# A two-layer streaming encoder on one core: inputs, input projection, queries and keys in one block written out by hand, and another order inside the delta stage

## The chip, the cores and the metric

The kernel runs on one core of one Trainium2 chip. The metric is the time of one execution on the device in microseconds (us), the median of the runs shown. The profile is one further execution of the same program. TensorE (PE) does the matrix products, ScalarE (ACT), VectorE (DVE) and GpSimd (POOL) the elementwise work, and SyncE (SP) issues the DMAs.

## What is computed

One inference step of a two-layer encoder for 1024 prompt tokens and 64 sample tokens that share the weights. Cut to what matters here:

```python
# layer 0, mixer
h = x @ w_in                                   # x (tokens, 1024), w_in (1024, 2208)
c_q, c_kv, k_r, gate_b, gate_c, sh = split(h)  # 384, 256, 32, 512, 512, 512
q   = rms_norm(c_q, g_q) @ w_uq                # 8 heads of 64 + 32; rope on the 32
lat = rms_norm(c_kv, g_kv)                     # output p_latent / s_latent
kr  = rope(k_r)                                # output p_krope / s_krope
kv  = concat(past_lat, lat) @ w_ukv            # keys and values of 8 heads
o_att = chunk_attention(q, k, v)
o_sc  = gate_b * causal_dwconv(gate_c * sh)    # 3 taps
x = layer_norm(ALPHA * x + concat(o_att, o_sc) @ w_o);  x = layer_norm(ALPHA * x + conv_ffn(x))
# layer 1, mixer: gated delta rule in chunks of 64 tokens, 8 heads of 128
#   per chunk: m = tril(k b k^T * decay), solve (I + m) sol = rhs, then
#   v_new = w - k_cd S;  o = q_dec S + attn v_new;  S = S g + k_tail^T v_new
```

All is float32. A product of float32 rank is made of three products of rounded parts: high by high, low by high, high by low.

## The kernel before

**Layout.** Features lie on the 128 partitions and tokens along the free dimension: 1092 columns (1024, a gap of 4, 64), in three thirds of 364 (`SPLIT`), each third one PSUM bank. `TILES` are nine tiles of 128 tokens (the last of 64). Every operand exists as a rounded part `hi` and a rest `lo`. `mm3` (lines 142 to 151) issues the three matmuls of one product. A *unit* of weights is 1024 x 128 numbers: SP loads it into `wraw` (three slots), POOL makes `whi` (L134) and `wlo` (L138) of it, and PE multiplies it with all tokens in 3 x 8 x 3 = 72 matmuls. The 18 units of the input projection are kv0, kv1, kr, q0, q1, q2 (the `head`) and four times gc, sh, gb.

**Blocks.** The program is a row of blocks; no engine goes into the next one before all have ended the present one. Semaphores of a block are cleared by POOL (L97) as the next one closes.

- `inputs_block`: SP issues 16 small loads of parameters, then nine tiles of x; PE waits for the small loads (`rows_in`), transposes them (L240), then transposes x, eight 128 x 128 pieces a tile (L253); ACT rounds the tile to `xhi` (L265), DVE subtracts to `xlo` (L273) and scales to `z` (L275). At the end all of `z` goes to the tensor `residual` in one DMA.
- `even_in_block`: the 18 units; ACT and DVE evacuate `ps`; DVE does the short convolution of each gc, sh, gb group (L539 to L563).
- `queries_block`: squares on ACT, sums over partitions with a matrix of ones on PE (L639), Sqrt on ACT (L617), reciprocal on DVE (L661), scaling (L664), `qhi` and `qlo`, 216 matmuls with `w_uq`, evacuated to `qT` (L628), and the rotation (rope) of `krf` and of each head on DVE: shuffle, two products, one sum (L684 to L690).
- `keys_block`: the cached latents are loaded and transposed (L754), the new ones are transposed back to rows and stored (L762, L835), then the keys (ACT to `kT` L814 and `kpast` L816) and the values (DVE to `V`, L839). POOL copies the rotated `krf` to the eight heads of `kT` (L743).
- `attention_block`, then `out_ffn_block` and a layer norm, then layer 1: `odd_in_block`, `gates_block`, `delta_block`, `out_ffn_block`, layer norm. The final layer norm writes the outputs.

**The delta stage.** `delta_block` walks over pairs of chunks. In one `run(A, B, C)` on each engine, pair A is prepared, pair B (the one before) is put through the state S, and the gates of C are made ready. The engines' programs are written out in a fixed order. For A: `kn` scales the keys (L2461), `gram_k` on PE fills bank 6, from which DVE makes `T` (L2468), `TT` (L2470), `MT` (L2471), and adds the identity to `TT` (L2476) and `T` (L2477); `AT` comes from bank 7 (L2480); `kturned` (L2222) transposes the keys into banks 6 and 7, from which DVE makes `ktl` (L2487) and ACT `kbg` (L2377). Then five levels: `X = T^T ML` (PE L2274, banks 4 and 5, copied by ACT L2388), then two products into banks 6 and 7 (L2287, L2290), which DVE subtracts from `T` and `TT` (L2504, L2505). For B: `vn` (L2442), a step of the state (PE L2185, DVE L2448), twice, and the squares of the output (ACT L2382). Before the first level PE waits for the second `S` (`pe.wait_ge(s("S"), B.th(3, 2))`).

## Time and profile before

| what | us |
|---|---|
| median of 3 runs (lowest, highest) | 3386.13 (3385.78, 3389.47) |
| the profiled execution's own time | 3385.98 |
| its span, first to last instruction | 3384.2 |
| PE busy | 3093.8 |
| POOL busy | 1053.3 |
| DVE busy | 1582.2 |
| ACT busy | 718.0 |

The span is the time between the first and the last instruction in the trace; 1.8 us lie around it. Busy times are sums of instructions and overlap between engines. The granted clock is the share of TensorE's full speed that it was allowed; half is 1.2 GHz, full is 2.4 GHz.

### The profile page before, as it was taken

The page shows a single profiled execution, that of the slowest core. Times are in us where ns is not written, and L with a number is a line of the kernel's source. Part 1 is how long each engine was busy: PE and PEld are TensorE (multiplying, and loading weights), DVE is VectorE, ACT ScalarE, POOL GpSimd, SP SyncE. Part 2 cuts the span into 40 slices and gives each one's busy share as a digit, 9 for nine tenths or more (in the row PEclk, how much of TensorE's full clock was granted, in tenths as well). Part 3 has the DMA queues.
Part 4 walks back from the last instruction along what each step waited for, and adds up shares of the span by engine and source line. Part 5 has one row for each costly group of instructions (what it writes and reads, how often), then busy time and mean ns, then how long its engine had stood idle before and what let it go on. Part 6 is the DMA issues. An engine that isn't in the chain of part 4 may idle for free. (4 is left out here: it accounts for less than half of the span.)

```text
span 3384.2 us, 54266 instructions
## 1 busy us (share of the span) xinstructions
PE 3093.8 (91%) x22776; PEld 2932.2 (87%) x22776; DVE 1582.2 (47%) x2716; ACT 718.0 (21%) x1349; POOL 1053.3 (31%) x708
## 2 busy tenths in 40 slices
PE   5997799999999999995999948988799999999996
PEld 4996666999999999983999947777689999999995
DVE  2127376463434434443666645555164444434444
ACT  1002267130010100103112224444031110100102
POOL 1220110343222233203232236666425233222220
PEclk8998899999999999997999979999799999999998
DMA  4100110211111111102233223331401111111101
GB/s 148 44 24 18 31 44 2 85 38 48 40 44 44 38 44 57 38 1 91 78 96 96 77 72 82 85 77 37 144 13 54 40 44 57 38 44 44 38 26 54
DMA packets 251736, 184.15 MB, mean 54 GB/s; under 512 B 47695, under 2 KB 236477, under 8 KB 251269
## 3 DMA queue, kind: packets, MB, share of 16 engines
q1 hardware_dynamic: 251525, 181.09, 17.9%
q8 instruction: 162, 2.65, 0.3%
q14 instruction: 49, 0.40, 0.0%
HBM read 147.19 MB, written 33.84 MB: 53 GB/s over the span
## 5 line engine op out<-in xcount | busy, mean ns | idle before, releaser
L145 PE MATMUL ps<-xhi,whi 128*128 128x364 f32 (+1 forms) x3528 | 1165.7, 330 | 88.0 <-POOL wlo L138 68.4
L146 PE MATMUL ps<-xlo,whi 128*128 128x364 f32 (+1 forms) x3528 | 1163.6, 330 | 0.0
L151 PE MATMUL ps<-xhi,wlo 128*128 128x364 f32 (+1 forms) x3528 | 1162.7, 330 | 0.0
L145 PEld LDWEIGHTS ps<-xhi,whi 128*128 128x128 f32 (+1 forms) x3528 | 662.0, 188 | 94.8 <-POOL wlo L138 69.1
L146 PEld LDWEIGHTS ps<-xlo,whi 128*128 128x128 f32 (+1 forms) x3528 | 662.2, 188 | 4.3 <-issue 0.8
L151 PEld LDWEIGHTS ps<-xhi,wlo 128*128 128x128 f32 (+1 forms) x3528 | 661.8, 188 | 3.4 <-issue 0.6
L1540 DVE TENSOR_TENSOR z<-ps,z 128x364 f32<-128x364 f32 x528 | 283.3, 537 | 640.3 <-PE ps L151 640.3
L1310 POOL TENSOR_SCALAR whi<-wraw 128x1024 fp32r<-128x1024 f32 x136 | 149.1, 1096 | 1036.2 <-PE ps L151 1034.6
L1313 POOL TENSOR_TENSOR wlo<-wraw,whi 128x1024 fp32r<-128x1024 f32 x136 | 349.0, 2566 | 11.3
L134 POOL TENSOR_SCALAR whi<-wraw 128x1024 fp32r<-128x1024 f32 (+3 forms) x56 | 57.0, 1019 | 497.2 <-PE ps L145 229.3
L145 PE MATMUL ps<-oo_hhi,whi 128*128 128x364 f32 x528 | 173.8, 329 | 0.3 <-DVE z L1540 0.3
L145 PE MATMUL ps<-eo_hhi,whi 128*128 128x364 f32 x528 | 173.8, 329 | 0.3 <-DVE z L1540 0.3
L151 PE MATMUL ps<-eo_hhi,wlo 128*128 128x364 f32 x528 | 173.6, 329 | 0.0
L151 PE MATMUL ps<-oo_hhi,wlo 128*128 128x364 f32 x528 | 173.6, 329 | 0.0
L146 PE MATMUL ps<-eo_hlo,whi 128*128 128x364 f32 x528 | 173.2, 328 | 0.0
L146 PE MATMUL ps<-oo_hlo,whi 128*128 128x364 f32 x528 | 173.2, 328 | 0.0
L138 POOL TENSOR_TENSOR wlo<-wraw,whi 128x1024 fp32r<-128x1024 f32 (+3 forms) x56 | 133.7, 2388 | 4.7
L1756 DVE SCALAR_TENSOR_TENSOR oin_conv<-oin_raw,par,oin_conv 128x1092 f32<-128x1092 f32 x72 | 109.0, 1514 | 10.5 <-DVE oin_conv L1752 0.2
L145 PEld LDWEIGHTS ps<-eo_hhi,whi 128*128 128x128 f32 x528 | 99.3, 188 | 0.6 <-DVE z L1540 0.6
L145 PEld LDWEIGHTS ps<-oo_hhi,whi 128*128 128x128 f32 x528 | 99.3, 188 | 0.6 <-DVE z L1540 0.6
L146 PEld LDWEIGHTS ps<-oo_hlo,whi 128*128 128x128 f32 x528 | 99.2, 188 | 0.0
L146 PEld LDWEIGHTS ps<-eo_hlo,whi 128*128 128x128 f32 x528 | 99.2, 188 | 0.0
(376 smaller groups left out, 4294.4 us busy)
## 6 DMA issues: line engine op xcount, KB each, us to landing
wraw<-in_w_ff_in SPq DMA_DIRECT2D x88, 512.0 KB, 3.8
wraw<-in_w_ff_out SPq DMA_DIRECT2D x44, 512.0 KB, 3.5
qkvz<-oin_out SPq DMA_DIRECT2D x32, 546.0 KB, 2.8
wraw<-in_w_in_o SPq DMA_DIRECT2D x32, 512.0 KB, 4.3
residual<-z SPq DMA_DIRECT2D x2, 4368.0 KB, 11.8
z<-residual SPq DMA_DIRECT2D x6, 1456.0 KB, 9.8
wraw<-in_w_in_e SPq DMA_DIRECT2D x17, 512.0 KB, 3.8
dn_gb<-gates SPq DMA_DIRECT2D x34, 128.0 KB, 3.4
```

The lines of the kernel that those rows point to most:

```text
L134: pool.tensor_scalar(m.whi[:, k, 0:cols], m.wraw[:, r, 0:cols], 1.0, 1.0, ALU.mult, ALU.mult)\
L138: pool.tensor_tensor(m.wlo[:, k, 0:cols], m.wraw[:, r, 0:cols], m.whi[:, k, 0:cols].bitcast(F32), ALU.subtract).then_inc(s("w_lo"), 1)
L145: one = pe.matmul(out, whi, xhi, start=start, stop=False)
L146: two = pe.matmul(out, whi, xlo, start=False, stop=False)
L151: return pe.matmul(out, wlo, xhi, start=False, stop=stop)
L1310: pool.tensor_scalar(hi, m.wraw[:, n % RAW, :], 1.0, 1.0, ALU.mult, ALU.mult).then_inc(s("w_hi"), 1)
L1313: pool.tensor_tensor(lo, m.wraw[:, n % RAW, :], hi.bitcast(F32), ALU.subtract).then_inc(s("w_lo"), 1)
L1540: dve.tensor_tensor(m.z[:, o, SPLIT[q]], m.ps[:, 6 + seq % 2, 0:NS], m.z[:, o, SPLIT[q]], ALU.add)\
L1756: dve.scalar_tensor_tensor(cv[:, :], x[:, 1 + t:1 + t + TW], one("dconv", t), cv[:, :], ALU.mult, ALU.add).then_inc(s("taps"), 1)
```

## The change

The blocks for inputs, input projection, queries and keys become one, `front_block`, with no loop in it. In it x is loaded first; after every three tiles of x one third of the unit kv0 is multiplied; the parameters come behind the first two units; `ALPHA * x` goes tile by tile through the buffer `zt` to `residual`. The latents' sums of squares are made by one matmul with ones each, after DVE has added the squares, and stand between the units, as do the transposes of the latents; the root is Exp(-0.5 Ln), with no reciprocal. The queries follow the last unit, the keys the queries (both now in two sets of banks), and the values the keys (four banks). Buffers share their places, so that some loads wait (the tables `cos` and `sin` for the short convolution's end). The rows of `kr` are turned and stored at once (`krows`).

In `delta_block` the first level's X goes to banks 0 and 1, ACT makes `vb` before `eg` and the squares of the output after the first X, DVE multiplies bank 6 in place and makes `T` from it in one sum out of PSUM, adds the identity to `TT` later, and PE starts `kcd` half by half.

```diff
--- before.py
+++ after.py
-def inputs_block(nc, ctx, m, d):
-def even_in_block(nc, ctx, m, d):
-def queries_block(nc, ctx, m, d):
-def keys_block(nc, ctx, m, d):
+def front_block(nc, outer, m, d):
...
+        PAIR = [4, 6, 2, 4, 6, 2, 4, 6, 4]
...
+            x_tile(0)
+            x_tile(1)
+            x_tile(2)
+            weight(0)
+            x_tile(3)
+            weight(1)
+            x_tile(4)
+            x_tile(5)
+            z_tile(0)
+            z_tile(1)
+            x_tile(6)
+            weight(2)
+            for t in (7, 8):
+                z_tile(t - 5)
+                x_tile(t)
...
+            sp.wait_ge(s("osc"), NT)
+            sp.wait_ge(s("st_done"), NT)
+            sp.dma_start(cos[rr, :], d["rope_cos"]).then_inc(s("tables"), 16)
+            sp.dma_start(sin[rr, :], d["rope_sin"]).then_inc(s("tables"), 16)
...
+            def turn_x(t):
+                n = TILES[t][1]
+                pe.wait_ge(s(f"x_in{t}"), 16)
+                if t >= 3:
+                    last = t - 3 if t < 8 else 6
+
+                    pe.wait_ge(s(f"zt{last % 2}"), last // 2 + 1)
+                for k in range(KD):
+                    ins = pe.transpose(tile_psum(t)[:, k, :], xin[0:n, t % 4, k * P:(k + 1) * P], m.ident[0:n, 0:n])
...
+            for t in (0, 1, 2):
+                turn_x(t)
+            pe.wait_ge(s("lo_x"), 3)
+            gemm(0, 0)
+            for t in (3, 4, 5):
+                turn_x(t)
+            pe.wait_ge(s("lo_x"), 6)
+            gemm(0, 1)
+            for t in (6, 7, 8):
+                turn_x(t)
+            pe.wait_ge(s("lo_x"), 9)
...
+            for n in range(2, NU):
+                for q in range(SPL):
+                    gemm(n, q)
+                if 3 <= n < 6:
+                    sum_of_squares(n - 3)
+                if 7 <= n < 10:
+                    sum_of_squares(n - 4)
+                if 8 <= n < 17:
+                    turn_latent(n - 8)
...
+                    elif h == 1:
+                        pe.wait_ge(s("q_free"), SPL * HEADS)
+                        if q == 2:
+
+                            pe.wait_ge(s("krows"), 1)
...
+            act.preload_act_table_set(LN_EXP)
+            for step in ("h0", "h1", "h2", "z0", "h3", "h4", "z2", "h5", "h6", "z4", "h7", "z6", "h8", "z8"):
+                (high if step[0] == "h" else scaled)(int(step[1]))
...
+            for t in range(9):
+                low(t)
+                if t % 2:
+                    scaled(t)
...
+            dve.wait_ge(s("tables"), 32)
+            for h in range(HEADS):
+                rope(h)
+            dve.wait_ge(s("kr_turned"), 1)
+            dve.tensor_copy(krows[:, 0:NTOK, :], m.ps[:, 6, 0:NTOK * ROPE].rearrange("p (t r) -> p t r", r=ROPE))
+            dve.tensor_copy(krows[0:DEC, NTOK, :], m.ps[0:DEC, 6, NTOK * ROPE:9 * ROPE]).then_inc(s("krows"), 1)
+            rope(HEADS)
...
+    X_BANK = [None, 0] + [4] * (LEVELS - 2)
...
                     if B:
-                        pe.wait_ge(s("S"), B.th(3, 2))
-                    else:
-                        pe.wait_ge(s("vb"), A.th(1, 1))
-
+                        pe.wait_ge(s("vn"), B.th(B.nb, 2))
                     for l in range(1, LEVELS):
                         pe.wait_ge(s("ML"), A.th(l, LEVELS - 1))
+                        if l == 2:
+
+                            if B:
+                                pe.wait_ge(s("S"), B.th(3, 2))
...
-                    pe.wait_ge(s("TT"), A.th(A.group(LEVELS - 1, A.nb - 1), 2 * LEVELS))
                     pe.wait_ge(s("vb"), A.th(1, 1))
...
                     for b in range(A.nb):
+                        pe.wait_ge(s("TT"), A.th(A.group(LEVELS - 1, b), 2 * LEVELS))
+                        settle(pe, s("settled_pe"))
...
-                if B:
-                    act.wait_ge(s("o"), B.th(len(B.blocks()), 2))
-                    act.activation(sq[:, :, 0:B.n], bank2(2, B.n), ACT.Square).then_inc(s("osq"), 1)
+                if B and not A:
+                    squares_o(B)
...
-                            act.copy(X[:, hs, :], bank1(4 + b)[:, hs, :]).then_inc(s("Xs"), 1)
+                            act.copy(X[:, hs, :], bank1(X_BANK[l] + b)[:, hs, :]).then_inc(s("Xs"), 1)
+                        if B and l == 1:
+                            squares_o(B)
```

On TensorE, at the start of the program, the order before is the following (`ptmp` holds the parameters' rows, `xin` the tiles of x; in brackets the semaphores waited for).

```order
L240 MATMUL ps<-ident,ptmp 128x114 [waits in_rows_in,in_consts]
L240 MATMUL ps<-ident,ptmp 128x66 x2
L240 MATMUL ps<-ident,ptmp 128x72
L240 MATMUL ps<-ident,ptmp 128x96
L240 MATMUL ps<-ident,ptmp 128x64
L253 MATMUL ps<-ident,xin 128x128 [waits in_x_in0]
```

At the same place now, with the first product right behind three tiles:

```order
L444 MATMUL ps<-ident,fr_xin 128x128 [waits fr_x_in0,fr_ident]
L444 MATMUL ps<-ident,fr_xin 128x128 x7
L444 MATMUL ps<-ident,fr_xin 128x128 [waits fr_x_in1]
L444 MATMUL ps<-ident,fr_xin 128x128 x7
L444 MATMUL ps<-ident,fr_xin 128x128 [waits fr_x_in2]
L444 MATMUL ps<-ident,fr_xin 128x128 x7
L145 MATMUL ps<-xhi,whi 128x364 [waits fr_w_lo,fr_lo_x]
```

The parameters no longer stand ahead of x, and the first matmul of kv0 waits for three tiles and its weights instead of nine tiles, the residual's store and a block's end.

On VectorE, in the part behind the last unit of the projection, the order now is this (`fr_osc` is the short convolution's result, `fr_llo` the latents' rest, `fr_turned` the rotation's buffer, `fr_tables` the semaphore of the loads of cos and sin).

```order
L787 TENSOR_TENSOR fr_osc<-fr_gc,fr_gb 128x1092 [waits fr_free0,fr_conv]
L846 TENSOR_TENSOR fr_plo<-ps,fr_phi 128x2x128 [waits fr_osc,fr_st_done,fr_past_hi]
L846 TENSOR_TENSOR fr_plo<-ps,fr_phi 128x2x128 [waits fr_past_hi]
L849 COPY strow<-ps 16x128 [waits fr_z_gap_out]
L853 TENSOR_TENSOR fr_llo<-fr_ckv,fr_lhi 128x1092 [waits fr_lat_turned,fr_lhi] x2
L799 STREAM_SHUFFLE fr_turned<-fr_krf 32x1092 [waits fr_tables]
L800 TENSOR_TENSOR fr_turned<-fr_krf,fr_cos 32x1092
L802 TENSOR_TENSOR fr_turned<-fr_turned,fr_sin 32x1092 [waits fr_swapped]
L805 TENSOR_TENSOR fr_krf<-fr_turned 32x1092 [waits fr_sind,fr_cosd]
```

Norms, reciprocals and `qlo` no longer stand between the last unit and the rotations, but the tables' loads and the latents' rest do.

On VectorE in a full `run` of the delta stage the order before is:

```order
L2468 TENSOR_TENSOR dn_T<-ps,dn_low 128x512
L2470 TENSOR_TENSOR dn_TT<-ps,dn_upl 128x512
L2471 TENSOR_TENSOR dn_MT<-ps,dn_ups 128x512
L2448 TENSOR_TENSOR dn_S<-ps,dn_Sg 128x1024
L2476 TENSOR_TENSOR dn_TT<-dn_TT,masks 128x512
L2477 TENSOR_TENSOR dn_T<-dn_T,masks 128x512
L2480 TENSOR_TENSOR dn_AT<-ps,dn_upi 128x512
```

The same place now:

```order
L2666 TENSOR_TENSOR dn_TT<-ps,dn_upl 128x512
L2667 TENSOR_TENSOR dn_MT<-ps,dn_ups 128x512
L2670 TENSOR_TENSOR ps<-ps,dn_low 128x512
L2645 TENSOR_TENSOR dn_S<-ps,dn_Sg 128x1024
L2675 TENSOR_TENSOR dn_T<-ps,masks 128x512
L2678 TENSOR_TENSOR dn_AT<-ps,dn_upi 128x512
L2639 TENSOR_TENSOR dn_vn<-dn_kbg,ps 128x512
L2682 TENSOR_TENSOR dn_TT<-dn_TT,masks 128x512
```

The sum that ends in `T` now reads PSUM, and the one that ends in `TT` has moved behind `AT` and the second `vn`.

## Rows read from the trace of the kernel before

**Rows 1.** The page: TensorE's busy tenths and granted clock in 40 slices

```profile
PE   5997799999999999995999948988799999999996
PEclk8998899999999999997999979999799999999998
```

**Rows 2.** Timeline, 0 to 60 us: start, duration, engine, what, [idle before <-releaser]

```profile
6.97 3.79 SPq L213 DMA_DIRECT2D xin<-in_x_prompt  x8
8.02 1.22 PE L240 MATMUL ps<-ident,ptmp 114*128 114x114 f32 x6 [8.02 <-DMA dtb<-in_dt_bias]
...
12.23 1.01 ACT L265 CAST xhi<-ps 128x1024 fp32r<-128x1024 f32 x1 [2.08 <-PE ps L253]
13.35 1.23 DVE L273 TENSOR_TENSOR xlo<-ps,xhi 128x1024 fp32r<-128x1024 f32 x1 [13.35 <-ACT xhi L265]
...
44.95 12.68 SPq L120 DMA_DIRECT2D wraw<-in_w_in_e  x6
...
49.13 1.04 POOL L134 TENSOR_SCALAR whi<-wraw 128x1024 fp32r<-128x1024 f32 x1 [2.80 <-DMA wraw<-in_w_in_e]
50.26 2.34 POOL L138 TENSOR_TENSOR wlo<-wraw,whi 128x1024 fp32r<-128x1024 f32 x1
...
52.65 0.67 PE L145 MATMUL ps<-xhi,whi 128*128 128x364 f32 x1 [27.06 <-POOL wlo L138]
```

**Rows 3.** One line each, evacuations of the units: min/median/max ns, first and last start

```profile
L506 ACT COPY ckv<-ps x3: 462/462/463, 59.1 to 67.1; 128x364 f32<-128x364 f32 x3
L517 ACT COPY ein_gb<-ps x12: 462/463/464, 154.9 to 270.7; 128x364 f32<-128x364 f32 x12
```

**Rows 4.** One line each, between the last unit and attention

```profile
L639 PE MATMUL ps<-q_sq,ones x30: 469/814/976, 276.8 to 300.4; 128*128 128x364 f32 x30
L628 ACT COPY qT<-ps x24: 457/459/462, 313.2 to 347.8; 96x364 f32<-96x364 f32 x24
L690 DVE TENSOR_TENSOR qT<-q_turned x8: 1286/1287/1289, 320.8 to 357.8; 32x1092 f32<-32x1092 f32 x8
L814 ACT COPY kT<-ps x24: 455/456/457, 379.7 to 408.5; 64x364 f32<-64x364 f32 x24
L839 DVE COPY V<-ps x11: 683/692/693, 410.6 to 424.5; 128x512 f32<-128x512 f32 x10, 64x512 f32<-64x512 f32 x1
L1023 ACT ACT_TABLE_LOAD  x1: 1283/1283/1283, 427.9 to 427.9; - x1
```

**Rows 5.** Timeline, 424 to 432 us: TensorE's first work in the attention block

```profile
425.54 0.62 PE L935 MATMUL ps<-kpast,qT 96*64 96x256 f32 x2 [1.05 <-PEq L702]
```

**Rows 6.** One line each: VectorE on two-input or SBUF work, beside GpSimd and alone

```profile
L563 DVE TENSOR_TENSOR osc<-ein_gc,ein_gb x4: 1297/1913/1915, 163.5 to 271.3; 128x1092 f32 x4
L743 POOL COPY kT<-krf x8: 1086/1090/1094, 373.6 to 380.9; 32x1092 f32<-32x1092 f32 x8
```

**Rows 7.** Timeline of the delta stage, 2140 to 2186 us, VectorE

```profile
2147.60 2.38 DVE L2477 TENSOR_TENSOR dn_T<-dn_T,masks 128x512 f32<-128x512 f32 x1
...
2153.15 1.22 DVE L2448 TENSOR_TENSOR dn_S<-ps,dn_Sg 128x1024 f32<-128x1024 f32 x1
```

**Rows 8.** The same stretch, TensorE, ScalarE and GpSimd

```profile
2150.84 1.06 PE L2222 MATMUL ps<-ident,dn_k 128*128 128x128 f32 x8 [0.46 <-DVE dn_AT L2480]
...
2154.51 1.15 PE L2274 MATMUL ps<-dn_T,dn_ML 64*64 64x64 f32 x32 [0.67 <-DVE dn_S L2448]
2156.43 0.95 PE L2287 MATMUL ps<-dn_X,dn_TT 64*64 64x64 f32 x16 [0.78 <-ACT dn_X L2388]
...
2174.48 2.00 PE L2305 MATMUL ps<-dn_TT,dn_kbg 64*128 64x64 f32 x32 [0.61 <-DVE dn_TT L2505]
...
2152.83 2.17 ACT L2377 ACTIVATE dn_kbg<-ps,bcol 128x128 f32<-128x128 f32 x8 [8.39 <-DVE dn_ktl L2487]
...
2147.08 2.35 POOL L2113 TENSOR_TENSOR dn_Sg<-dn_S,dn_egl 128x1024 f32<-128x1024 f32 x1
```

**Rows 9.** Windows: length, busy (x instructions) PE, PEld, DVE, ACT, POOL, clock, DMA, GB/s

```profile
2061.12:2101.22 40.10, 36.28 (x730) 31.83 (x730) 23.03 (x35) 20.39 (x42) 28.22 (x18) 1.00 0.31 81
```

More of the change, by code:

```diff
@@ new lines, in gemm @@
+            def gemm(n, q):
+                kind, t = UNITS[n]
+                g, i = group(UNITS[n])
+                cols = wide(kind)
+                hi, lo = halves_of(n)
+                pe.wait_ge(s("w_lo"), n + 1)
+                if i >= 1:
+                    pe.wait_ge(s(f"free{g}"), SPL * (i - 1) + q + 1)
+                for k in range(KD):
+                    w = slice(k * cols, (k + 1) * cols)
+                    ins = mm3(pe, m.ps[0:cols, 3 * g + q, 0:NS], hi[:, w], lo[:, w], m.xhi[:, k, SPLIT[q]],
+                              m.xlo[:, k, SPLIT[q]], k == 0, k == KD - 1)
+                ins.then_inc(s(f"full{g}"), 1)
@@ L262, in _ @@
             ins.then_inc(s("params_done"), 1)
[L263 to L265 removed]
+            evacuate(("kr", 0), krf[rr, :])
+            squares(0)
+            root(0)
+            squares(1)
+            evacuate(("q", 1), cq[:, 1, :])
+            root(1)
+            squares(2)
+            root(2)
+            squares(3)
+            gate(0)
+            root(3)
@@ new lines, in _ @@
+            squares(4)
+            evacuate(("gb", 0), gb)
+            root(4)
+            squares(5)
+            latent_row(0)
+            gate(1)
+            root(5)
+            for k in range(KKV):
+                act.wait_ge(s("normed"), normed_count(SPL))
+                act.copy(lhi[:, k, :], ckv[:, k, :]).then_inc(s("lhi"), 1)
+            latent_row(1)
+            for k in range(KQ):
+                act.wait_ge(s("normed"), normed_count(2 * SPL))
+                act.copy(qhi[:, k, :], cq[:, k, :]).then_inc(s("qhi"), 1)
```

904 lines of the change are left out of this document (486 added, 418 removed).

## The prediction

> **What bounds the kernel now.** I read the page first. TensorE's row of tenths shows a 5 in the first slice of 84.6 us and two 7s in the fourth and fifth, then 9 nearly throughout up to the last third; it is the engine that the rest waits for [rows 1]. So I looked for its holes and for what ends them.
>
> The timeline of the first 60 us gives the first hole. The small loads stand ahead of x in SP's queue: x is issued at 6.97, TensorE starts at 8.02 behind the last small load, ACT rounds the first tile at 12.23. The first product starts at 52.65, after 27 us of idleness that the weights' `wlo` ends; the weights were issued only at 44.95, once the residual had been stored and the block had ended [rows 2]. From there to the last unit TensorE has no hole: the evacuations of a unit's thirds come 4.0 us apart (59.1 to 67.1 is two steps), so a unit costs 12.0; the first third costs more, since 52.65 to 67.1 is 14.45 for what takes 12.0 later (clock at half: 2.4 us) [rows 2, 3].
>
> The second hole lies between 270.7 (last evacuation of the last unit) and 425.5 (first work of attention): 154.8 us [rows 3, 5]. The lines in it show what it holds: sums of squares to 300.4, the first query evacuated at 313.2, the last at 347.8, rotations to 357.8 and 1.3 more, the first key evacuated at 379.7, the last at 408.5, values to 425.2 [rows 4]. The products alone are 36 + 30 + 16 us; some 70 us are waits in a row.
>
> The third is the delta stage. One full pair takes 40.1 us with TensorE busy for 36.3 [rows 9]. Its own waits in a pair are short: 0.46, 0.67, 0.78 and 0.61 us [rows 8], but what it does in between is stretched by an order in which VectorE's chain comes first.
>
> **The change, part by part.**
>
> *Head.* x is issued first, at about 0.8. From issue to rounding it takes 12.23 - 6.97 = 5.3, so the first rounding is at 6.1; the last of three tiles needs 1.0 on ACT and four steps of VectorE (three `xlo`, one scaled tile) of 1.2 [rows 2]: 12.0. The weights are fourth in the queue: 4.2 from issue to GpSimd's start before (44.95 to 49.13), some 8.3 now, and 1.04 + 2.34 for the split gives 11.7 [rows 2]. First third 12.0 to 16.0. The next three tiles are turned only then: 1.1 for eight transposes (1.06 for eight of this size in [rows 8]), 1.0, and four steps of 1.2: product at 22.9 to 26.9. The last three tiles are in series with the scaling that frees their banks and with the store that frees `zt` (an ACT step, a transposition, an ACT step, and about 3 us for a store): 9.8, product at 36.7. Two thirds of a unit (8.0) being done, it is as if the projection had begun at 28.7, against 52.65: **24.0 us** gained. The half-speed start of 2.4 is paid in both.
>
> *Between the units* TensorE gets six sums at 0.47 (the shortest of L639) [rows 4], 2.8, six parameter transposes (0.8) and 18 latent transposes (0.13 each by [rows 8] and a start for each of nine pairs, estimated at 3.2): 6.8 us added. Their partners on ACT and VectorE have a whole unit of 12 us each; the longest queue ahead of one (convolution, product, norm, sum after gb0) is some 9 us by durations like those in [rows 6], so I cost their waits at nothing; without that cover each would cost its excess over 12.
>
> *Behind the last unit*, at U: five transposes, 1. Queries: 34.6 us for 23 steps [rows 4], 1.5 each, 24 of them, 36.1: U+37.1. Small transposes: U+38.7. A head of keys takes 3.7 (28.8 us for nearly eight, less the slow start) [rows 4]; head 0 and two thirds of head 1 end at U+44.4, and there TensorE waits for `krows`, which stands behind eight rotations on VectorE. Those: the convolution's last product beside GpSimd 1.9 [rows 6], from U+0.7, so U+2.6 (the tables, issued then, land by about U+5.5); the past's rests and the copy 1.2; the latents' two rests 1.3 each and 0.6 each lost beside GpSimd's split, U+7.6. A rotation comes every 5.28 us (37.0 / 7 in L690) [rows 4], eight are 42.3. GpSimd makes its eight copies of 1.09 into `kT` meanwhile [rows 6]; about five two-input steps fall into that time and lose 0.6 each (1.91 against 1.30) [rows 6]: 3. With two copies 0.5: U+53.4. So TensorE stands for 9.0 us, and what was late next is the keys: 24.1 left, 2.0 for a clock at half after the pause, U+79.5; values 15.9 as before, 0.3 to attention: U+95.7. With the 6.8 that is 102.5 against 154.8: **52.3** gained. What is gone here are norms, reciprocals, Sqrt, two block ends, two loads and a row-by-row store.
>
> The first exponential of attention no longer waits for its table, 1.28 [rows 4]: **1.3**.
>
> *Weighing a rule.* The sum into `T` takes 2.38 us for 512 columns, where `S` out of PSUM takes 1.22 for 1024; it starts while GpSimd's `Sg` runs from 2147.08 to 2149.43 and ends 0.55 after it [rows 7, 8]. The Trainium skill, SBUF — State Buffer, section "Who interferes with whom", says that a VectorE instruction with two SBUF inputs is fully blocked by a GpSimd instruction that reads SBUF, and that one with a single SBUF input is not. By this rule the new sum out of PSUM is free of it, and the trace agrees with the 2.38. It speaks against the front, though: five rotation steps would each lose a copy's 1.09, not 0.6, and `krows` come 2.5 later; the total would be 3289 instead of 3286.
>
> *Delta.* Relative to `kn` at 2141.20. VectorE: `TT`, `MT`, the in-place product and `T` out of PSUM at 0.7 each (an estimate from 1.22 for `S`, twice as wide), the last in place of 2.38 [rows 7], `AT`, `vn`: the second `vn` comes about 1.8 earlier. But TensorE's own queue was done only 0.46 before `kturned` at 2150.84 [rows 8]; the earlier `vb` moves that queue by some 0.4 more, so only 0.8 of the 1.8 arrives there, at 2150.0. `kbg` then starts at 2152.0 instead of 2152.83. Level one no longer waits for the second `S` (end of 2153.15 + 1.22): it starts near 2153.0, not 2154.51, and ACT copies X before it squares B's output, which takes about 1 us out of the 1.4 between `kbg`'s end (2155.0) and the next product. `kbg` ends at 2154.1, X is copied by 2154.5, the next product starts there instead of at 2156.43: **1.9**. `kcd` waits for the first half of `TT` alone: the wait of 0.61 goes [rows 8]. 2.5 per pair; eight full stages 20, the first stage (no B) about 2: **22**. `TT`'s identity sum, two SBUF inputs, now stands beside GpSimd; it may lose up to 1.3, and the 1.0 between it and `kturned` hides most of that. GpSimd is busy 28 of 40 us [rows 9]; everything it does starts as much earlier.
>
> Sum: 24.0 + 52.3 + 1.3 + 22 = 99.6. From the profiled execution's 3385.98: **3286**; that execution lies 0.15 under the median of the runs, so the figure stands for it too.
>
> **Rivals.**
> - *Better tail and steadier clock* (0.22): the pause at `krows` is as short as the rotations alone make it (4.8 off), no half clock behind it (2.0), and the added transposes are paid by half (3); delta gains 3 per pair. Another 13: 3273. For it: the stretches with a full clock in [rows 1]. Against: TensorE's pauses of this size were followed by half speed at 52.65 [rows 2, 3].
> - *Delta gives little* (0.15): the pair is held by TensorE's own 36.3 of 40.1 [rows 9]; if only the waits shown go (0.61 + 0.67), 8 x 1.3 = 10. 12 less: 3298.
> - *A slower head* (0.10): x, nine stores of 512-byte pieces and weights share SP's queue, and TensorE works in bursts there, so half speed is paid for two thirds more (2 x 4) and a store or load comes 4 late: 3298.
> - *Slower than before* (0.02): the small steps between the units drop the clock to 1.2 GHz for the projection. A unit then costs 24 instead of 12 (the half-speed start shows matmuls taking twice as long). From 8.3 of the 18 units on, the whole gain is gone; with all of them the time is 3502. Against it: the projection runs at full clock through [rows 1]'s third slice, and the added steps are 0.5 us.
> - *It does not do what it says* (0.01): the steps between the units are held by ACT's and VectorE's queues, 15 of them at 6.6 us each, about the 100 that the rest gives: 3386. For it: ACT and VectorE each serve all of them in one order. Against: a unit's 12.
> - My forecast as worked out, 3278 to 3294: 0.50.
>
> **How the numbers follow.** The likeliest case gives 3286. The range reaches over the better tail and over the two weaker cases: 3267 to 3304; outside I leave 2 in 10. 0.2% is 6.8 us, about what a measurement of this kernel tells from none; all cases but two are far beyond it on the fast side: faster 0.97, same 0.01, slower 0.02.
>
> **What would show it.** In the changed profile: first L145 near 12 us, with holes behind each third until about 37; no hole longer than 1 us from there to the last unit near 253; a wait for `krows` of 5 to 11 us about 44 us behind it; attention's first matmul near 349; `dn_T` out of PSUM at 0.7 us and a pair every 37.5 us. I am wrong if TensorE waits at the sums between the units, if half clock shows inside the projection, or if the pair stays at 40.

## The result and the profile after

The changed kernel takes 3305.93 us (median of 4 runs, 3305.22 to 3307.16) against 3387.8 for the kernel before (4 runs beside them, 3385.78 to 3389.59): ratio 0.9753, 95% interval 0.974 to 0.9767. It is 82 us faster, where I had forecast 100: the time lies 20 us above the 3286 and just above my range. The profiled execution's span fell from 3384.2 to 3304.5, by 79.7; the accounts below are made with spans.

The page's two rows for TensorE look like those of [rows 1]; only the start is better filled.

```profile
PE   7998999999999999985999949998899999999996
PEclk8999999999999999997999979998899999999998
```

The timeline of the first 50 us shows what took the place of the hole of [rows 2]: three bursts of products, each behind a pause.

```profile
4.91 4.68 PE L444 MATMUL ps<-ident,fr_xin 128*128 128x128 f32 x24 [4.91 <-DMA fr_xin<-in_x_prompt]
...
13.18 0.67 PE L145 MATMUL ps<-xhi,whi 128*128 128x364 f32 x1 [3.60 <-DVE xlo L724]
...
19.89 1.91 PE L444 MATMUL ps<-ident,fr_xin 128*128 128x128 f32 x16
...
27.39 0.67 PE L145 MATMUL ps<-xhi,whi 128*128 128x364 f32 x1 [2.36 <-DVE xlo L724]
...
33.86 1.03 PE L444 MATMUL ps<-ident,fr_xin 128*128 128x128 f32 x8
...
42.49 1.02 ACT L604 ACTIVATE fr_zt<-ps 128x1024 f32<-128x1024 f32 x1 [3.37 <-DMA residual<-fr_zt]
43.66 1.09 PE L444 MATMUL ps<-ident,fr_xin 64*128 64x64 f32 x8 [5.58 <-ACT fr_zt L604]
...
46.15 0.67 PE L145 MATMUL ps<-xhi,whi 128*128 128x364 f32 x1 [1.40 <-DVE xlo L724]
```

The thirds of the first unit begin at 13.18, 27.39 and 46.15 (forecast 12.0, 22.9, 36.7). The first two last 6.7 and 6.5 us, not 4.0. The windows over the same stretch (busy time of PE, PEld, DVE, ACT, POOL, then PEclk, DMA share, GB/s) say why: the clock is near its half level, 1.2 GHz, in both.

```profile
13.00:20.00 7.00, 6.82 (x25) 6.80 (x26) 0.13 (x1) 0.00 (x0) 3.16 (x2) 0.57 1.14 284
20.00:27.00 7.00, 2.87 (x25) 2.42 (x23) 4.38 (x4) 3.87 (x4) 1.14 (x2) 0.91 0.31 77
27.00:34.00 7.00, 6.61 (x26) 6.58 (x27) 1.56 (x2) 0.00 (x0) 0.00 (x0) 0.60 0.87 228
```

The waits of TensorE between the last unit (its last product ends at about 261.9) and the start of attention:

```profile
PE ps L145 <- DVE fr_krows L860: 13.0, 1, 13.0
PE ps L1139 <- ACT att_p L1213: 3.3, 1, 3.3
PE ps L1125 <- PEq L256: 1.1, 1, 1.1
```

I had 9.0 for the first and nothing for the second. Added up by stretches of the two spans (forecast, measured):

| stretch | forecast | measured | missed |
|---|---|---|---|
| start to the last unit's end | ends at 253.5 | 261.9 | 8.4 |
| last unit to attention's first product | 95.7 | 98.5 | 2.8 |
| attention to its last result | 1.3 gained | 171.8 against 168.6, 3.2 lost | 4.5 |
| attention's last result to the first `kn` | nothing | 1431.6 against 1428.5 | 3.1 |
| first to last `kn` (delta) | 22 gained | 302.1 against 322.0, 19.9 gained | 2.1 |
| last `kn` to the end | nothing | 1038.6 against 1039.6 | -1.0 |

The misses add up to 19.9, and 99.6 - 19.9 is the 79.7.

### The profile page after: what moved, and what is told of

Read it like the earlier page. It is cut to its first block and busy times, and to the rows that moved or that the text cites. A ratio compares the mean times of both kernels' runs of the same rounds, so it can differ in the third digit from the quotient of the medians.

```text
span 3304.5 us, 54021 instructions
## 1 busy us (share of the span) xinstructions
PE 3082.5 (93%) x22758; PEld 2930.9 (89%) x22758; DVE 1582.0 (48%) x2701; ACT 722.6 (22%) x1346; POOL 1062.7 (32%) x708
## 5 line engine op out<-in xcount | busy, mean ns | idle before, releaser
L1503 POOL TENSOR_TENSOR wlo<-wraw,whi 128x1024 fp32r<-128x1024 f32 x136 | 349.4, 2569 | 11.3
L134 POOL TENSOR_SCALAR whi<-wraw 128x1024 fp32r<-128x1024 f32 (+1 forms) x33 | 34.7, 1052 | 248.6 <-DMA wraw<-in_w_in_o 132.0
L151 PEld LDWEIGHTS ps<-oo_hhi,wlo 128*128 128x128 f32 x528 | 99.1, 188 | 0.0
```

Source lines behind the costliest of these rows:

```text
L134: pool.tensor_scalar(m.whi[:, k, 0:cols], m.wraw[:, r, 0:cols], 1.0, 1.0, ALU.mult, ALU.mult)\
L151: return pe.matmul(out, wlo, xhi, start=False, stop=stop)
L1503: pool.tensor_tensor(lo, m.wraw[:, n % RAW, :], hi.bitcast(F32), ALU.subtract).then_inc(s("w_lo"), 1)
```

## The experiments

Sixteen kernels. "Changed" is the kernel under study at 3305.93 us; medians are of 4 or 5 runs. Two things limit how finely they can be read: the same head code brings the last unit's end to anywhere from 258.6 to 261.9, and eleven kernels with the same new delta stage have stretches from first to last `kn` of 301.4 to 307.5 us (mean 304.3). Below 3 us I read nothing from one profile. The changed kernel's own profile is at the late end of that head, so comparisons of the head with it flatter what they test. And the kernel before, run again beside each group of experiments, had medians of 3389.55 to 3392.85 us where it had 3387.8 beside the changed kernel: a difference of two medians from different groups is uncertain by 2 to 5 us, and the ratios, each taken against the kernel before in its own group, are the better guide there.

| label | us | ratio to before (95%) | span |
|---|---|---|---|
| e_delta | 3367.92 | 0.9938 (0.9917 to 0.9959) | 3366.0 |
| e_front | 3327.89 | 0.9818 (0.98 to 0.9835) | 3322.5 |
| e_krows | 3290.01 | 0.9705 (0.9687 to 0.9724) | 3287.1 |
| e_gap | 3299.32 | 0.9735 (0.9717 to 0.9753) | 3294.4 |
| e_order | 3303.35 | 0.9742 (0.9729 to 0.9756) | 3301.6 |
| e_zbuf | 3302.04 | 0.9739 (0.9725 to 0.9752) | 3300.3 |
| e_warm | 3300.39 | 0.9731 (0.9718 to 0.9745) | 3300.2 |
| e_kg | 3283.32 | 0.9683 (0.967 to 0.9696) | 3279.8 |
| e_eo | 3301.74 | 0.9734 (0.9718 to 0.9751) | 3298.3 |
| e_best | 3271.42 | 0.9641 (0.9624 to 0.9657) | 3270.7 |
| e_noT | 3304.76 | 0.9744 (0.9727 to 0.976) | 3305.7 |
| e_noX | 3315.8 | 0.9774 (0.9755 to 0.9793) | 3313.9 |
| e_dve | 3312.12 | 0.9768 (0.9755 to 0.9782) | 3309.9 |
| e_noVB | 3309.02 | 0.9754 (0.974 to 0.9767) | 3307.6 |
| e_noKCD | 3309.36 | 0.9758 (0.9744 to 0.9771) | 3311.2 |
| e_pool | 3298.18 | 0.9724 (0.971 to 0.9737) | 3301.7 |

**The two halves: e_delta and e_front.** The edit is the function `delta_block` of one kernel in the other, nothing else.

> The kernel before with the delta stage of the changed one and nothing else. The stretch from the first kn to the last was 19.9 us shorter in the changed kernel's trace. If the delta orders are worth that by themselves, and the front only shifts them: 19 to 22 us under the kernel before, about 3367. Rival: part of the 19.9 came with the clock or with what the front leaves behind, then the two parts do not add up and this gives 12 or less.

> The changed kernel with the delta stage of before, so the new front alone. If the parts add up: 3306 + 20 = 3326, 61 us under the kernel before, where my prediction had 24.0 + 52.3 + 1.3 = 77.6. Rival: the front is worth its 77.6 and it is the two together that lose 16 us; then this gives about 3310.

By spans the delta stage alone gives 18.2 and the front alone 61.7: 79.9 together, against 79.7 for both at once. The ratios say the same (21 and 62 us of 3387.8). They add up, the rivals (12 us or less, and about 3310) are out, and the miss lies in the front: 61.7 where I had 77.6. That the sum agrees to 0.2 is chance: e_delta's head came 2.1 later than in the kernel before with the same instructions, and e_front's last unit ended 3.3 earlier than the changed kernel's.

**The stall at `krows`: e_krows.**

```diff
-            for h in range(HEADS):
+            for h in range(5):
                 rope(h)
             dve.wait_ge(s("kr_turned"), 1)
...
-            rope(HEADS)
+            for h in range(5, HEADS + 1):
+                rope(h)
```

> The changed kernel with the two copies of krows on VectorE put behind the fifth rotation instead of the ninth-but-one; the rotations themselves and everything else as they are. Theory: TensorE's 13.0 us of idleness behind the second head's keys is the queue ahead of these copies; the fifth rotation ends at 301.5, TensorE needs the bank at 304.7, so the 13.0 goes, and 1 to 2 us of half clock behind it: 13 to 15 us faster than the changed kernel, about 3292. Rival: what is late next (the last rotations, the copies of the keys on ACT, GpSimd's copies) takes most of it: 3299 or more.

The copies now run at 300.8, the wait for `fr_krows` is gone from the list of waits, and from the last unit to attention it takes 83.1 us instead of 98.5: 15.4 less: 13.0 of wait, and 2.4 for the clock, which was granted at 0.50 and 0.65 from 316 to 324 us behind the wait and is at 1.00 throughout now. The median is 16 lower. Nothing takes the stall's place.

**A part of why the stall was 13.0 and not 9.0: e_pool.**

```diff
-            pool.wait_ge(s("roped"), 1)
+            pool.wait_ge(s("roped"), HEADS)
             for h in range(HEADS):
                 pool.tensor_copy(m.kT[rr, h, :], krf[rr, :]).then_inc(s("kr"), 1)
```

> The changed kernel with GpSimd's eight copies of the turned key rows waiting for the eighth rotation, so that no rotation runs beside them. In the changed kernel the first two query rotations and part of the third take 2.0 to 2.2 us a step where the later ones take 1.28: seven steps lose 5.2 us together, where I had put 3. Theory: the krows copies come 5.2 us earlier and the pause of 13.0 us on TensorE shrinks to 7.8; the copies are done long before attention: 5 us faster, 3301. Rival: GpSimd is still splitting weights beside the rotations, or its copies now hold the V memset and with it the values: no gain.

The timeline of the changed kernel: one of GpSimd's copies beside VectorE's shuffle and three beside its next steps (each asked for by itself; the timeline of a longer stretch merges them), the rotation of VectorE beside them, and one later:

```profile
276.04 1.09 POOL L426 COPY kT<-fr_krf 32x1092 f32<-32x1092 f32 x1 [3.89 <-DVE fr_krf L805]
...
278.12 2.16 POOL L426 COPY kT<-fr_krf 32x1092 f32<-32x1092 f32 x1
280.23 2.15 POOL L426 COPY kT<-fr_krf 32x1092 f32<-32x1092 f32 x1
282.33 2.16 POOL L426 COPY kT<-fr_krf 32x1092 f32<-32x1092 f32 x1
...
277.34 1.98 DVE L800 TENSOR_TENSOR fr_turned<-qT,fr_cos 32x1092 f32<-32x1092 f32 x1
279.25 2.18 DVE L802 TENSOR_TENSOR fr_turned<-fr_turned,fr_sin 32x1092 f32<-32x1092 f32 x1
281.53 2.00 DVE L805 TENSOR_TENSOR qT<-fr_turned 32x1092 f32<-32x1092 f32 x1
...
292.32 1.27 DVE L800 TENSOR_TENSOR fr_turned<-qT,fr_cos 32x1092 f32<-32x1092 f32 x1
293.52 1.28 DVE L802 TENSOR_TENSOR fr_turned<-fr_turned,fr_sin 32x1092 f32<-32x1092 f32 x1
294.90 1.29 DVE L805 TENSOR_TENSOR qT<-fr_turned 32x1092 f32<-32x1092 f32 x1
...
317.32 0.43 DVE L859 COPY fr_krows<-ps 128x256 f32<-128x256 f32 x1
```

And of the kernel with the copies later, the first query rotation and the wait:

```profile
277.26 1.27 DVE L800 TENSOR_TENSOR fr_turned<-qT,fr_cos 32x1092 f32<-32x1092 f32 x1
278.46 1.28 DVE L802 TENSOR_TENSOR fr_turned<-fr_turned,fr_sin 32x1092 f32<-32x1092 f32 x1
```

```profile
PE ps L145 <- DVE fr_krows L860: 8.6, 1, 8.6
```

The stall shrank by 4.4 where I expected 5.2; the way from the last unit to attention by 3.8, the median by 7.8. The missing 0.8 is the seventh slow step, which I had put down to the copies: it is the rotation of `krf` at 271.21, beside GpSimd's last splitting of weights, and it takes 2.06 us in e_pool too. The third query rotation was not slowed in either. So the copies slow six steps and cost 4.4, where the prediction had put 3 for five; that part of `krows`' lateness is shown.

**Attention's start: e_gap.**

```diff
         def _(dve):
...
             masks, adds = [0], [0]
+            for hp in range(HP):
+                dve.memset(attended(hp)[:, SEQ:S0], 0.0).then_inc(s("gap"), 1)
...
         def _(pool):
-            for hp in range(HP):
-                pool.memset(attended(hp)[:, SEQ:S0], 0.0).then_inc(s("gap"), 1)
```

> The changed kernel with attention's four small memsets of the gap columns moved from GpSimd to the head of VectorE's program. Theory: ACT's first exponential at 366.13 waits for these memsets, and they stand on GpSimd behind some 70 clears of the front's semaphores (360.3 to 365.9); without it the exponential starts about 3.3 to 4.5 us earlier: 3301.5 to 3302.7. Rival: something else that GpSimd's or the block's end holds (scores, maximum) is due at the same time: no difference, 3306.

In the kernel before the first exponential starts 3.70 us behind TensorE's first product at 425.54, its table's 1.28 included:

```profile
429.24 0.52 ACT L1023 ACTIVATE att_p<-ps,att_ng 64x320 f32<-64x320 f32 x1
```

In the changed kernel's timeline it waits for a memset of four columns, which GpSimd reaches 5.5 us after TensorE has begun:

```profile
360.40 0.62 PE L1125 MATMUL ps<-fr_kpast,qT 96*64 96x256 f32 x2 [1.05 <-PEq L256]
...
365.99 0.11 POOL L1334 MEMSET att_o<- 128x4 f32 x1
366.13 0.52 ACT L1213 ACTIVATE att_p<-ps,att_ng 64x320 f32<-64x320 f32 x1 [21.72 <-POOL att_o L1334]
...
366.89 1.06 PE L1139 MATMUL ps<-ident,att_p 64*128 64x64 f32 x6 [3.29 <-ACT att_p L1213]
```

With the memsets on VectorE the exponential follows the maximum at once:

```profile
359.30 0.62 PE L1125 MATMUL ps<-fr_kpast,qT 96*64 96x256 f32 x2 [1.05 <-PEq L256]
...
361.72 0.52 ACT L1213 ACTIVATE att_p<-ps,att_ng 64x320 f32<-64x320 f32 x1 [18.42 <-DVE att_ng L1273]
...
364.83 1.06 POOL L1337 TENSOR_SCALAR whi<-wraw 128x1024 fp32r<-128x1024 f32 x1 [42.67 <-issue]
```

It starts 2.4 us behind TensorE's first product instead of 5.7; from that product to attention's last result it takes 166.4 instead of 171.8: 5.4, of which 3.3 is the wait and 2.1 the clock behind it (granted at 0.52 and 0.50 from 367 to 373 us, at 1.00 in e_gap). GpSimd still does nothing else for 5.5 us (359.3 to 364.8). What it does there is the clearing of the front's semaphores (`Sems.close`, L97). The clears of this place, in the changed kernel and then in the kernel before:

```profile
L97 POOLq EVENT_SEMAPHORE_RANGE_CLEAR  x78: 44/44/48, 360.3 to 365.8; - x78
```

```profile
L97 POOLq EVENT_SEMAPHORE_RANGE_CLEAR  x22: 44/44/44, 425.5 to 426.9; - x22
```

78 clears take 5.5 us and 22 took 1.4.

**Both: e_kg.** The two edits together.

> Both moves together on the changed kernel: the copies of krows behind the fifth rotation, and attention's gap memsets on VectorE. Alone they measured 16 to 17 us and 6 to 10 us (spans 3287.1 and 3294.4 against 3304.5), of which I take 15.4 and 5.4 as theirs, by the stretches that they touch, and the rest as chance of the head's clock. If they are independent: 21 us under the changed kernel, span about 3283.5. Rival: both live off the same pause of TensorE, and together they give no more than the first alone, 3290.

22.6 by median, 24.7 by span, where 21 was expected. The two stretches are as in the kernels with one edit each: 83.2 us from the last unit to attention (83.1 in e_krows), 166.3 through attention (166.4 in e_gap). They are independent; the rest of the 24.7 is spread of the head and of other stretches.

**The head: e_order, e_zbuf, e_warm.** The first moves one step of ACT, and on SP the small loads behind the residual's stores; the second gives each of the nine scaled tiles its own buffer (on ACT, VectorE and SP alike); the third puts 108 transposes of the identity into six holes of TensorE, 26, 12, 14, 12, 36 and 8 of them (the first place is shown).

```diff
-            for step in ("h0", "h1", "h2", "z0", "h3", "h4", "z2", "h5", "h6", "z4", "h7", "z6", "h8", "z8"):
+            for step in ("h0", "h1", "h2", "z0", "h3", "h4", "z2", "h5", "z4", "h6", "h7", "z6", "h8", "z8"):
```

```diff
-                if t >= 2:
-                    act.wait_ge(s("z_out0"), 16 * (t // 2))
-                act.activation(zt[:, 0, :, 0:n], tile_psum(t), ACT.Copy, scale=ALPHA).then_inc(s("zt0"), 1)
+                act.activation(z_buf(t), tile_psum(t), ACT.Copy, scale=ALPHA).then_inc(s("zt0"), 1)
```

```diff
+            def warm(bank, n):
+                for _ in range(n):
+                    pe.transpose(m.ps[:, bank, 0:P], m.ident[:, :], m.ident[:, :])
...
             for t in (0, 1, 2):
                 turn_x(t)
+            warm(0, 26)
             pe.wait_ge(s("lo_x"), 3)
             gemm(0, 0)
```

> The changed kernel with two moves in the head: ACT scales tile 4 ahead of rounding tile 6 (not behind it), and SP issues the sixteen small loads behind the residual's stores (not ahead of tile 4's). Theory: the third group of tiles is late because the scaled tiles queue up behind their stores, two buffers deep; tile 4's store then goes out some 6 us earlier, and the second unit third's product starts at 40 to 42 instead of 46.2: 4 to 6 us faster, 3300 to 3302. Rival: the stores are held by the 16 DMA engines, not by their place, and land no earlier: within 2 us of 3306.

> The changed kernel with a buffer of its own for each of the nine scaled tiles (in memory that the query latents take later), so that no scaling waits for a store; orders on all engines unchanged. Theory: with the two DMA waits of 3.37 and 3.70 on ACT and VectorE gone, x's last tile is turned at about 40.3 and the third product starts near 43 instead of 46.2: 3 to 4 us faster, about 3302.5. Rival: what is late there is the clock and the order, not the store: under 1.5 us.

> The changed kernel with 108 transposes of the identity by itself put into TensorE's six holes between 8 and 46 us (26, 12, 14, 12, 36 and 8 of them), into banks that the next product overwrites; nothing waits for them. Theory: the thirds of the first unit take 6.7 and 6.5 us instead of 4.0 because the clock is at half behind each hole; with TensorE busy in the holes they run at full clock and 5 to 7 us of the head go: about 3300. Rival: the clock falls whatever fills the holes, or the fillers themselves come in the way: 3306 or more.

The third product starts at 41.51, 41.38 and 41.55 instead of 46.15. But in the other kernels with the head unchanged it starts anywhere from 42.82 (e_front) to 45.99 (e_pool), so that only 1.3 us of the 4.6 is sure to come from the edit. The last unit ends at 258.0 and 257.0 for the first two, against 258.6 to 261.9; the medians fell by 2.6 and 3.9, less than the 4 to 6 that I gave the order. What is shown is the wait itself: in e_order ACT's scaling of tile 6 waits 0.80 us for a store, not 3.37 (1.7 to 3.1 in the other kernels); in e_zbuf not at all. With the holes filled the windows over the changed kernel's three stretches become:

```profile
13.00:20.00 7.00, 7.00 (x52) 6.98 (x52) 0.83 (x1) 1.88 (x3) 3.05 (x2) 1.00 1.15 276
20.00:27.00 7.00, 5.31 (x40) 4.86 (x39) 3.88 (x4) 1.99 (x3) 1.13 (x2) 1.00 0.74 206
27.00:34.00 7.00, 6.24 (x51) 5.94 (x50) 2.51 (x3) 2.95 (x3) 0.00 (x0) 1.00 0.66 147
```

The granted clock is 1.00 throughout, the first product lasts from 12.94 to about 17.0, the second starts at 24.55, and the last unit ends at 255.7 instead of 261.9, and 2.9 before the earliest of the unchanged heads. So half clock behind the pauses is shown as the greatest part of the head's miss: in the first two thirds alone 5.2 of the 8.4. By median it gives 5.5; its delta stretch happened to be one of the longest, 307.5.

**The pause behind attention: e_eo.** The same filler, 28 times, behind attention's last product.

```diff
             for g in range(NU + 1):
...
                     weigh(LAST_OF.index(g - 1))
+            for _ in range(28):
+                pe.transpose(m.ps[:, 0, 0:P], m.ident[:, :], m.ident[:, :])
```

> The changed kernel with 28 transposes of the identity behind attention's last product, in the pause of 3.6 us before the output projection; nothing waits for them. Theory: the pause is the same in all runs, but the half clock behind it lasts 2 to 6 us depending on when the pause falls, and that is a part of the 3.2 us which the changed kernel loses between attention and the delta stage; filled, the stretch from attention's last result to the first sum of the projection (14.7 us in the changed kernel, 13.4 before) comes to 11.5 to 12, and the whole is 2 to 3 us faster: 3303. Rival: the slow products there have another cause, the stretch stays 14.7.

The pause of TensorE there is 3.56 in the kernel before and 3.55 in the changed one. The windows behind it, first of the kernel before:

```profile
597.00:600.00 3.00, 2.67 (x9) 2.70 (x10) 0.01 (x1) 1.28 (x1) 0.78 (x3) 0.50 0.42 90
600.00:603.00 3.00, 3.00 (x19) 3.00 (x18) 0.00 (x0) 0.00 (x0) 2.92 (x3) 0.97 1.03 379
```

then of the changed kernel:

```profile
535.00:538.00 3.00, 2.60 (x9) 2.63 (x10) 0.08 (x1) 1.28 (x1) 0.70 (x3) 0.50 0.36 85
538.00:541.00 3.00, 3.00 (x12) 3.00 (x10) 0.00 (x0) 0.00 (x0) 2.92 (x3) 0.50 1.05 390
```

and with the filler:

```profile
533.00:536.00 3.00, 2.65 (x18) 2.44 (x17) 0.53 (x1) 1.28 (x1) 0.26 (x3) 1.00 0.22 36
536.00:539.00 3.00, 3.00 (x20) 3.00 (x19) 0.00 (x0) 0.00 (x0) 2.92 (x2) 1.00 1.04 379
```

The same products take 9 and 19 a window, 9 and 12, or 18 and 20. From attention's last result to the first sum it takes 13.4, 14.7 and 12.1. That the half clock behind the pause makes up the 2.6 is shown; that the difference of 1.3 between the two kernels comes from where the pause falls fits these rows and is not tested. The median is 4.2 lower, a little more than this stretch's 2.6.

**All of it: e_best.** The edits of e_krows, e_gap, e_order, e_zbuf, e_warm (with 26, 12, 14, 0, 18 and 10 fillers) and e_eo.

> All that helped, on the changed kernel: krows copies behind the fifth rotation, gap memsets on VectorE, own buffers for the nine scaled tiles, tile 4 scaled early and the small loads last, transposes of the identity in TensorE's holes of the head, and 28 more of them behind attention's last product. From the run with the first two (span 3279.8): the filled holes moved the last unit's end 6.2 us forward (255.7 against 261.9), and with buffers and order too the third product should start near 35.5 instead of 41.5, another 6; the pause behind attention gives 1.3 to 2.9. That is span 3265 to 3267. Rival: the stores now press together on the DMA engines, where weights and x wait too, and the head gives under 8 in all: 3271 or more.

3271.42 by median, 34.5 us under the changed kernel and 119 under the kernel before in its group (3390.79). The three thirds start at 12.92, 24.52 and 35.24, and the last unit ends at 249.4. The head gave 11.3 against e_kg's 260.7, the pause 1.4; 2.5 went again in a long delta stretch (307.3), and so the span is 3270.7, not 3266. The rival had named this range (3271 or more) for stores that press on each other and a head that gives under 8; the head gave 11.3.

**The delta stage in parts: e_noT, e_noX, e_dve, e_noVB, e_noKCD.** Each puts one part back as it was before.

```diff
-                    dve.tensor_tensor(bank1(6)[:, 0:J], bank1(6)[:, 0:J], low[:, 0:J], ALU.mult).then_inc(s("Ta"), 1)
+                    dve.tensor_tensor(T[:, 0:J], bank1(6)[:, 0:J], low[:, 0:J], ALU.mult).then_inc(s("Ta"), 1)
...
-                    dve.tensor_tensor(T[:, 0:J], bank1(6)[:, 0:J], masked(m.EYE, J), ALU.add).then_inc(s("T0"), 1)
+                    dve.tensor_tensor(T[:, 0:J], T[:, 0:J], masked(m.EYE, J), ALU.add).then_inc(s("T0"), 1)
```

> The changed kernel with the delta stage's T made in memory again: the masked product goes from PSUM to memory, and the identity is added there, beside GpSimd. My prediction gave this part 0.8 us a pair: 8 x 0.8 = 6.4 slower, 3312. Rival: the part was the greater share of the 19.9 (1.7 us of VectorE's chain in each of eight pairs reach TensorE whole): 13 slower, 3319.

```diff
-    X_BANK = [None, 0] + [4] * (LEVELS - 2)
+    X_BANK = [None] + [4] * (LEVELS - 1)
...
-                        pe.wait_ge(s("vn"), B.th(B.nb, 2))
+                        pe.wait_ge(s("S"), B.th(3, 2))
```

> The changed kernel with level one of the delta stage as before: its product X goes to the bank that waits for the state's second sum, and ACT squares the earlier pair's output ahead of it. My prediction gave level one and the order on ACT what is left of 1.9 us a pair once T's 0.8 is off: 1.1 x 8 = 9 slower, 3315. Rival: without the wait for the state's sum another one of VectorE (dn_X is waited for 6.8 us over nine pairs already) ends the gap just as late: under 3 slower.

e_dve has all of VectorE's old lines, the sum into `TT` ahead of `AT` among them; e_noVB puts ACT's exponential and copy ahead of `vb` again; e_noKCD waits for both halves:

```diff
+                    pe.wait_ge(s("TT"), A.th(A.group(LEVELS - 1, A.nb - 1), 2 * LEVELS))
...
                     for b in range(A.nb):
-                        pe.wait_ge(s("TT"), A.th(A.group(LEVELS - 1, b), 2 * LEVELS))
```

> The changed kernel with VectorE's whole order in the delta stage as before: T and TT from PSUM to memory, both identity sums in memory, ahead of AT. With T alone put back the stretch from the first kn to the last grew by 0.9 only (303.0 against 302.1), where I had predicted 6.4. Theory: what counted is the sum into TT, which stood ahead of AT and now stands behind it; TensorE waited 7.0 us for AT in eight pairs before and not at all now. Then this is 6 to 9 us slower than the changed kernel, about 3313. Rival: VectorE's order is worth nothing at all, since TensorE's own queue ends as late: under 2.

> The changed kernel with ACT's order before vb as it was: the decay's exponential and copy ahead of vb. TensorE waited 4.6 us for vb in seven pairs before, not at all now. Theory: those 0.65 us a pair are on the path: 4 to 5 us slower, 3311. Rival: TensorE then only comes earlier to the next wait (kturned, kbg): under 2, as my prediction had it (0.4 a pair, 3).

> The changed kernel with the kcd products waiting for both halves of TT again. My prediction took the whole wait of 0.61 us a pair from it: 8 x 0.61 = 4.9 slower, 3311. Rival: TensorE needs the second half 0.5 us later in any case and the wait is only partly gone: 1 to 2.

From first to last `kn`, against the mean of 304.3 for the new orders and 322.0 and 322.9 for the old (before, e_front): e_noT 303.0, e_noX 314.4, e_dve 311.3, e_noVB 306.6, e_noKCD 308.8. So `T` out of PSUM alone is worth nothing that shows; level one is worth 10 (a part of it clock, three of its pairs have a mean of 0.95), VectorE's whole order 7, the halves of `TT` 4.5; `vb` 2.3 and not certain. Each is one profile; e_noX and e_dve lie outside the spread of 301.4 to 307.5 clearly, e_noKCD by 1.3, and by device time no ratio of the five is clear of the changed kernel's (0.974 to 0.9767). They add up to 24 where all together give 18: some cover the same time, or it is the spread.

e_noT was meant to bring back the sum into `T` of 2.38 us [rows 7], and did not. Its sum has both inputs in memory again and takes 0.68 all the same, because now it starts before GpSimd's `Sg`, which then takes 2.27 instead of 1.90:

```profile
2042.99 0.68 DVE L2675 TENSOR_TENSOR dn_T<-dn_T,masks 128x512 f32<-128x512 f32 x1
```

```profile
2043.15 2.27 POOL L2304 TENSOR_TENSOR dn_Sg<-dn_S,dn_egl 128x1024 f32<-128x1024 f32 x1 [0.65 <-DVE dn_S L2645]
```

In e_dve the sum into `TT` (0.85) stands ahead of it again, `T`'s starts at 2044.23, behind `Sg` at 2043.72, and takes 2.38. It is the order of the two sums that shortened it, not PSUM. The waits that come back are those that were named: for `AT` in e_dve, for `vb` in e_noVB, for `TT` in e_noKCD, one line from each list of TensorE's waits.

```profile
PE ps L2413 <- DVE dn_AT L2678: 8.9, 8, 3.5
```

```profile
PE ps L2376 <- ACT dn_vb L2561: 5.0, 7, 0.8
```

```profile
PE ps L2497 <- DVE dn_TT L2704: 5.5, 9, 0.6
```

The wait for `vb` of 5.0 us lengthened the stretch by 2.3, if that is not spread; the rival (TensorE then only comes sooner to its next wait) fits, and is not shown further.

## Why the prediction was wrong, step by step

- **Head** (24.0 forecast, 8.4 too much). The step that failed is "the half-speed start of 2.4 is paid in both": it is paid in each of the three thirds. Two of them ran 2.7 and 2.5 us longer than the 4.0 that I used; e_warm removes this and the last unit comes 6.2 earlier. The rest is 1.2 and 0.6 in the starts of the first two and 2.5 in the third's chain of scaling and storing (12.3 us, not 9.8): there "about 3 us for a store" was too little, tile 4's store was issued at 36.90 and freed its buffer for ACT at 42.49. From the third product to the last unit's end it took 1.1 less than I had. A part of this is chance: with the same head the same store took 3.9 us in e_front (35.01 to 38.95) and the last unit ended at 258.6, which would have been a miss of 5.1. I had this case as the rival *a slower head*; it was the mechanism, and belonged into the sum, since the trace of before showed half clock behind a pause.
- **Between the units**: right. The six sums (two matmul records each, of 0.467 us) and the transposes show no wait, and no half clock.
- **Behind the last unit** (2.8 too much). The mechanism was right, the stall at `krows` with nothing late behind it. Its size was the term "about five two-input steps fall into that time and lose 0.6 each (1.91 against 1.30) [rows 6]: 3": six steps lost 4.4 to the copies, one more lost 0.8 beside the splitting of weights, and TensorE reached the bank 1.6 earlier than U+44.4. 9.0 became 13.0. From the copies on, 42.6 against my 42.3.
- **The rule weighed.** The rotation steps beside GpSimd's copies took 1.71 to 2.19 against 1.27 to 1.29, a loss of 0.4 to 0.9. The copies took 1.09 beside the shuffles, which read one tensor, and 2.15 to 2.17 beside the other steps, which read two. They take turns: the step issued at 277.34 ends at 279.32, the copy issued at 278.12 ends at 280.28, the next step at 281.43, the next copy at 282.38, each 0.95 to 1.15 behind the other's end. The Trainium skill, SBUF — State Buffer, section "Who interferes with whom", calls what they share "an exclusive lock", and the trace agrees. My price by the rule was wrong: a step does not lose a whole copy of 1.09, since the copy is under way when the step is issued; it lost 0.73 in the mean. In sum 4.4, against the 5.5 that I had worked out by the rule and the 3 that I took.
- **Attention** (1.3 gained forecast, 3.2 lost). The step that failed is the one that I left out: I costed the block's end at nothing. The front's block takes the place of four, GpSimd clears its 78 semaphores at its end (5.5 us; 22 and 1.4 before), and the memset that gates the first exponential stands behind them. e_gap shows it; there the exponential starts 2.42 us behind TensorE's first product instead of the 3.70 of the kernel before, the 1.3 that I had forecast, and attention is 2.2 shorter than before.
- **Attention's end to delta** (nothing forecast, 3.1 lost). 1.3 of it is the half clock behind the same pause of 3.6 us lasting longer (by the windows under e_eo); 1.3 more lies up to the first layer norm, where I saw such a difference behind another pause and tried nothing; 0.5 I can't place.
- **Delta** (22 forecast, 19.9 measured, 18 by the means). The sum was near, the reason of its first term not. I took the shorter sum into `T` for what reading PSUM gives, "free of it" by the rule weighed. It did fall from 2.38 to 0.68, but e_noT has 0.68 with both inputs in memory: what freed it is that `TT`'s sum no longer stands ahead of it, so that it starts before GpSimd's `Sg` instead of behind it. What the operand spares is GpSimd: `Sg` beside this sum takes 1.90 in the changed kernel and 2.27 in e_noT. `TT`'s sum stands beside GpSimd now and takes 1.79 for 0.83, a loss of 1.0 that nothing waits for. I also left the 0.8 of `TT`'s sum out of "about 1.8 earlier": from VectorE's first product of `gram_k` to `AT` it takes 3.7 us for 6.0. Of these 2.3 a pair TensorE got some 0.9 (e_dve, 7 over the stretch), near the "only 0.8" that I had, so this size was luck. Level one (9 forecast, 10) and the halves of `TT` (4.9 forecast, 4.5) came out as sized, within a spread of 3.
- The rival *slower than before*, half clock all through the projection, did not come: windows of the changed kernel from 60 to 261 us all have a granted clock of 1.00.

The rows of both sums in the changed kernel (duration in ns, least, median and most; first and last start):

```profile
L2675 DVE TENSOR_TENSOR dn_T<-ps,masks x9: 415/681/692, 1969.9 to 2270.9; 128x512 f32<-128x512 f32 x8, 128x256 f32<-128x256 f32 x1
...
L2682 DVE TENSOR_TENSOR dn_TT<-dn_TT,masks x9: 992/1793/1798, 1971.1 to 2272.9; 128x512 f32<-128x512 f32 x8, 128x256 f32<-128x256 f32 x1
```

## What to carry to other kernels

Where the trace of before shows half clock behind a pause of TensorE, count it behind every pause like it that the change makes, not once for a stage; where the pause can't go, cheap products that nothing waits for can keep the clock, and here they paid for themselves. Before crediting a faster instruction on VectorE to its operands, look which of VectorE and GpSimd starts first: here swapping two sums did what the move to PSUM was meant to do. When blocks are joined, ask what stands at the new end (semaphores to clear, stores to await) and what the next block's first step waits for on that engine. For a small copy that frees a bank, put it on its engine where it is first needed, not where its loop ends: that one move was worth 15.4 us, as much as the head gave (15.6).

## What the runs showed of the hardware

- Transposes of the identity by itself (26 of them in 3.00 us) held the granted clock at 1.00 over stretches in which it otherwise fell to 0.57 and 0.60.
- VectorE steps with two inputs in memory (32x1092) and GpSimd copies of the same size took turns, one instruction each: a step of 1.27 took up to 2.19 us and a copy of 1.09 took 2.16. Whichever started first was not slowed (the sum into `T`: 0.68 ahead of `Sg`, 2.38 behind it).
- 78 semaphore clears on GpSimd took 5.5 us, 70 ns each, though each is listed with 44 ns.
- The same pause of 3.55 to 3.56 us was followed by half clock of about 3 us in one program and 6 in another; the stretch over it took 13.3 to 13.5 us in five kernels (the one before, e_delta, e_order, e_kg, e_pool) and 14.2 to 14.8 in the others without the filler. What sets it is not shown; it makes differences of 1 to 2 us between kernels that do the same there.
- In the delta stage, kernels with the same instructions differ by up to 6 us over nine pairs; windows of a pair with a mean clock of 0.95 in place of 1.00 stand in the longer ones. Their cause stays open.
